# An attention and SSD encoder layer on one core: gated attention written over its gate, V in places of its own, decays loaded in halves, a new order in each head, and the first output step's operands rounded earlier

## The reference, cut to what matters

```python
h = rmsnorm(x, pre_norm_g)
proj = h @ w_in                      # 2048 -> 13376 columns: q, k, v, z_attn, z_ssm, x/B/C, dt
o = dilated_attention(q, k, v, rel_bias_table)          # 16 heads x 128
attn_out = rmsnorm(o, attn_norm_g) * silu(z_attn)
ssm_out = ssd_branch(z_ssm, xbc, dt_raw, ...)           # 32 heads x 64, both directions
mix = concatenate([attn_out, ssm_out]) @ w_out
y = x + rmsnorm(mix, post_norm_g)
```

## Time and profile before

| what | us |
|---|---|
| runs, median (lowest to highest) of 3 | 2471.28 (2469.89 to 2485.74) |
| the profiled execution's own time | 2472.09 |
| its span in the profile | 2470.3 |
| PE busy | 2409.2 (98%) |
| DVE busy | 1786.7 (72%) |
| ACT busy | 995.1 (40%) |
| mean granted TensorE clock | 0.993 of full |

### The profile page before, as it was taken

One profiled execution on the slowest core, in us unless ns is written; L12 is line 12 of the kernel. 1 busy time (PEld: TensorE's weight loads), 2 busy tenths in 40 slices (PEclk: granted clock), 3 DMA queues, 4 the chain that ended last, 5 costly groups with the idle time before them and its releaser, 6 DMA issues. The chain is left out here.

```text
span 2470.3 us, 36360 instructions
## 1 busy us (share of the span) xinstructions
PE 2409.2 (98%) x13604; PEld 2280.5 (92%) x13604; DVE 1786.7 (72%) x2563; ACT 995.1 (40%) x1664; POOL 466.1 (19%) x750
## 2 busy tenths in 40 slices
PE   7999999999999999999999999999999999999998
PEld 7999999999999999999998889899889888888887
DVE  5676766666666677777758778777878768777867
ACT  6333433333333333333335455454545532333332
POOL 0000277777773011111100000000000000000000
PEclk9999999999999999999999999999999999999999
DMA  5235466666665344443474555556555435445544
GB/s 167 72 112 182 126 198 206 204 205 200 200 199 158 114 128 132 127 125 119 122 242 145 184 184 160 182 179 193 156 192 167 139 133 170 151 156 130 175 160 164
DMA packets 318345, 398.81 MB, mean 161 GB/s; under 512 B 22822, under 2 KB 238310, under 8 KB 315287
## 3 DMA queue, kind: packets, MB, share of 16 engines
q1 hardware_dynamic: 266103, 225.20, 29.8%
q0 software_dynamic: 29168, 95.62, 12.2%
q10 hardware_dynamic: 22960, 76.53, 9.0%
HBM read 309.02 MB, written 95.59 MB: 164 GB/s over the span
## 5 line engine op out<-in xcount | busy, mean ns | idle before, releaser
L1166 PE MATMUL ps<-h_hi,w_hi 128*128 128x384 f32 x1088 | 365.2, 336 | 0.0
L1166 PE MATMUL ps<-h_lo,w_hi 128*128 128x384 f32 x1088 | 365.0, 335 | 0.0
L1166 PE MATMUL ps<-h_hi,w_lo 128*128 128x384 f32 x1088 | 364.6, 335 | 0.0
L2443 DVE TENSOR_TENSOR w_lo<-raw_qk,w_hi 128x512 fp32r<-128x512 f32 x272 | 214.3, 789 | 154.6 <-ACT w_hi L1696 153.2
L1166 PE MATMUL ps<-t_hi,w_lo 128*128 128x384 f32 x816 | 276.0, 338 | 0.0
L1166 PE MATMUL ps<-t_hi,w_hi 128*128 128x384 f32 x816 | 275.6, 338 | 0.0
L1166 PE MATMUL ps<-t_lo,w_hi 128*128 128x384 f32 x816 | 275.0, 337 | 0.0
L1696 ACT ACTIVATE w_hi<-raw_qk 128x512 fp32r<-128x512 f32 x272 | 171.2, 630 | 244.7 <-PE ps L1166 244.7
L1030 PE MATMUL ps<-h_hi,w_hi 128*128 128x384 f32 x768 | 205.2, 348 | 0.0
L1166 PEld LDWEIGHTS ps<-h_lo,w_hi 128*128 128x128 f32 x1088 | 204.3, 188 | 0.0
L1166 PEld LDWEIGHTS ps<-h_hi,w_lo 128*128 128x128 f32 x1088 | 204.2, 188 | 0.0
(11 more groups left out here) (370 smaller groups left out, 5411.9 us busy)
## 6 DMA issues: line engine op xcount, KB each, us to landing
raw_qk<-in_w_in SPq DMA_DIRECT2D x102, 512.0 KB, 4.3
w_raw<-in_w_in SPq DMA_DIRECT2D x144, 256.0 KB, 3.5
stage<-loc_scr ACTq DMA_DIRECT2D x16, 1536.0 KB, 11.9
stage<-t_scr SPq DMA_DIRECT2D x48, 512.0 KB, 3.8
stage<-zx_scr ACTq DMA_DIRECT2D x61, 384.0 KB, 5.2
stage<-in_w_out SPq DMA_DIRECT2D x36, 512.0 KB, 3.7
stage<-in_w_in SPq DMA_DIRECT2D x34, 512.0 KB, 4.2
zx_scr<-w_raw SPq DMA_DIRECT2D x34, 384.0 KB, 3.3
```

Source lines behind the costliest of these rows:

```text
L1166: ins = nc.tensor.matmul(ps[:, bank, 0:HALF_T], w, h(k), start=(start and kk == 0 and q == 0), stop=(last and kk == KC - 1 and q == 2), sk ...
L2443: nc.vector.tensor_tensor(w_lo[:, n_slot(n, pp), :], src, w_hi[:, n_slot(n, pp), :].bitcast(f32), ALU.subtract).then_inc(w_lo_done, 1)
```

## The change

It has five parts.

1. `attention_gated` writes its product over the gate `za` instead of over `oT`, and `store_att` stores `za`. The wait of `biased_maxima` for `ua_stored` goes. The load of the next `za` moves from `load_head` to `load_behind_scores`, behind a wait for `ua_stored`.
2. V is loaded in two halves into places of its own, and a head earlier, behind `v_rounded`.
3. The decays are loaded in two halves, one for each direction: the second half behind `silu_of_gates` of the head before (it waits for `wmat_done`, when that half of `decay` has been used), the first still behind `within_chunks`.
4. The order in a head: on PE `scores` stand one half earlier, two halves instead of one stand between `turn_probs` and `turn_probs_of_sample`, and three instead of two between `turn_v` and `across_chunks`. ACT and DVE are reordered to match.
5. The first output step: the `u` parts are rounded once the last gate tile's first chunk has been used, the weight pieces after its third, and the squares, `square_added`, `attention_gated` and `across_read` change places around them.

```diff
+        v_part = (sq_c[:, P:P + HALF_T], loc_ssum[:, TT * 64:TT * 64 + HALF_T])
...
-                pool.dma_start(u_scr[a * P:(a + 1) * P, :], oT).then_inc(ua_stored, 16)
+                pool.dma_start(u_scr[a * P:(a + 1) * P, :], za).then_inc(ua_stored, 16)
...
             def head(a):
-                stream_halves(a, 1, 2)
+                stream_halves(a, 1, 1)
                 scores(a)
                 scores_of_sample(a)
-                stream_halves(a, 3, 4)
+                stream_halves(a, 2, 4)
                 turn_probs(a)
-                stream_halves(a, 7, 1)
+                stream_halves(a, 6, 2)
                 turn_probs_of_sample(a)
                 attend(a)
+                stream_halves(a, 8, 1)
                 turn_x(a)
-                stream_halves(a, 8, 2)
                 if a < LAST:
                     turn_v(a + 1)
-                stream_halves(a, 10, 2)
+                stream_halves(a, 9, 3)
                 across_chunks(a)
...
-            def load_decays(a):
-                act.dma_start(decay.rearrange("p (d n) -> p d n", d=2),
-                              loc_scr.rearrange("(d h) t -> d (h t)", d=2)[:, a * 2 * T:(a + 1) * 2 * T]
+            def load_decays(a, d):
+                if a > 0 and d == 1:
+                    act.wait_ge(wmat_done, a)
+                act.dma_start(decay[:, 2 * T * d:2 * T * (d + 1)].rearrange("p (o n) -> p o n", o=1),
+                              loc_scr.rearrange("(d h) t -> d (h t)", d=2)[d:d + 1, a * 2 * T:(a + 1) * 2 * T]
                               .partition_broadcast(P)).then_inc(decay_in, 16)
...
-                load_decays(a)
-                if a < LAST:
-                    act.wait_ge(att_gated, a)
-                    load_zx(za, ZX_ZA, a, za_in)
+                load_decays(a, 0)
...
                     if a > 0:
+                        act.wait_ge(ua_stored, 16 * a)
+                        load_zx(za, ZX_ZA, a, za_in)
...
             def biased_maxima(a):
                 dve.wait_ge(strip_in, 16 * a + 16)
-                if a > 0:
-                    dve.wait_ge(ua_stored, 16 * a)
...
-                nc.vector.tensor_tensor(oT, oT, za, ALU.mult).then_inc(att_gated, 1)
+                nc.vector.tensor_tensor(za, oT, za, ALU.mult).then_inc(att_gated, 1)
```

More of the change, by code:

```diff
@@ L1636, in sample_rounded, with load_v @@
                 nc.scalar.activation(pTs_hi[:, :], ps[:, 4, :], ACT.Copy).then_inc(pts_out, 1)
[L1638 to L1641, removed]
+            def load_v(i):
+                for half in range(2):
+                    act.dma_start(v_part[half], zx_scr[(ZX_V + i) * P:(ZX_V + i + 1) * P,
+                                                       half * HALF_T:(half + 1) * HALF_T]).then_inc(v_in, 16)
             def attended(a):
@@ L1826, in head @@
                 probs_rounded(a)
+                exp_of_decays(a)
                 sample_rounded(a)
[L1828 to L1839, removed]
                 if i % 2:
                     k_rounded(i)
+                stream_hi(m + 2)
+                attended(a)
+                attended_sample(a)
+                squared(a)
+                stream_hi(m + 3)
+                x_turned(a)
+                v_rounded(i)
+                if a > 0:
+                    load_xs(i)
+                if i < LAST:
+                    load_v(i + 1)
+                if i % 2 == 0:
+                    q_rounded(i)
+                silu_of_gates(a)
+                load_decays(i, 1)
                 stream_hi(m + 4)
-                silu_of_gates(a)
+                stream_hi(m + 5)
                 if i % 2:
                     q_rounded(i)
-                stream_hi(m + 5)
-                if i % 2 == 0:
+                else:
                     k_rounded(i)
@@ L1869, in split_first_parts, with first_w2_rounded @@
                                      scale=mix_cols[:, kt:kt + 1]).then_inc(m_hi_done, 1)
+            def first_w2_rounded(k):
+                act.wait_ge(w2_in[0], 16)
+                nc.scalar.activation(w2_hi[0][:, k * NBW:(k + 1) * NBW], w2_first[:, k * NBW:(k + 1) * NBW], ACT.Copy
+                                     ).then_inc(w2_piece_hi, 1)
             load_head(LAST)
@@ L1876, in _ @@
             probs_rounded(LAST)
+            exp_of_decays(LAST)
             sample_rounded(LAST)
-            exp_of_decays(LAST)
             square_first(1)
             square_first(2)
+            last_gate_used(0)
+            for k in range(GRP):
+                first_u_rounded(k)
             attended(LAST)
+            attended_sample(LAST)
+            x_turned(LAST)
+            act.wait_ge(ua_stored, 16 * LAST)
             tile_ready(tile_of("za", LAST))
             tile_into(tile_of("za", LAST), parity_of("za", LAST), za, ACT.Silu)
-            x_turned(LAST)
-            attended_sample(LAST)
             squared(LAST)
+            last_gate_used(2)
+            for k in range(GRP):
+                first_w2_rounded(k)
             square_first(3)
             act.wait_ge(tile_done, tile_of("zs", LAST) + 1)
-            for k in range(GRP):
-                split_first_parts(k)
-                if k == 0:
-                    act.wait_ge(usq_added, 3)
-                    tile_into(tile_of("zs", LAST), parity_of("zs", LAST), zs, ACT.Silu)
+            act.wait_ge(usq_added, 3)
+            tile_into(tile_of("zs", LAST), parity_of("zs", LAST), zs, ACT.Silu)
             w2_split(1)
@@ L2596, in head @@
                 probs_lo(a)
-                if i % 2 == 0 and a < LAST:
-                    q_lo_of(i)
-                stream_lo(m)
+                stream_lo(m + 1)
+                if a == LAST:
+                    first_square()
                 sample_lo(a)
-                stream_lo(m + 1)
-                stream_lo(m + 2)
                 weighted_decays(a)
+                if a < LAST:
+                    square_added(a)
+                weights_in_chunks()
+                if a == LAST:
+                    add_square_first(1)
+                    add_square_first(2)
                 scaled_x(a)
                 if a == LAST:
-                    weights_in_chunks()
                     return
                 v_lo_of(i)
-                square_added(a)
-                weights_in_chunks()
+                if i % 2 == 0:
+                    q_lo_of(i)
+                stream_lo(m + 2)
                 stream_lo(m + 3)
@@ L2642, in split_first_parts, with first_w2_lo @@
                     m_hi[0][:, k * T:(k + 1) * T].bitcast(f32), ALU.mult, ALU.subtract).then_inc(m_lo_done, 1)
-            dve.wait_ge(u_first_in, 16)
-            nc.vector.tensor_tensor(ssum, u_first[0], u_first[0], ALU.mult).then_inc(usq_added, 1)
-            add_square_first(1)
-            add_square_first(2)
+            def first_w2_lo(k):
+                dve.wait_ge(w2_piece_hi, k + 1)
+                nc.vector.tensor_tensor(w2_lo[0][:, k * NBW:(k + 1) * NBW], w2_first[:, k * NBW:(k + 1) * NBW],
+                                        w2_hi[0][:, k * NBW:(k + 1) * NBW].bitcast(f32), ALU.subtract
+                                        ).then_inc(w2_piece_lo, 1)
+            for k in range(GRP):
+                first_u_lo(k)
+                first_w2_lo(k)
             square_added(LAST)
             attention_gated(LAST)
+            across_read(LAST)
             add_square_first(3)
-            for k in range(GRP):
-                split_first_parts(k)
-            across_read(LAST)
             skip_added(LAST)
```

42 lines of the change are left out of this document (21 added, 21 removed).

## The result

The changed kernel takes 2501.07 us (median of 4 runs, 2487.48 to 2506.45), the kernel before 2471.32 beside it (4 runs, 2469.89 to 2485.74): ratio 1.0098, interval 1.0051 to 1.0144. It is about 1% slower, where 2429 was forecast, and lies outside the range of 2422 to 2448.

A forecast was written before the change was run, and what follows sets the result against it. PE, busy 98% of the span, was taken to lose time only by 39.3 us of waits and a lowered clock. Gains of 35.7 and 12.3 made 48.0, less 6 paid back, net 42: 2429.3 us, range 2422 to 2448.

The forecast's parts named there:

- I take 7: Decays' load in the head loop: a 768 KB half was taken to land 7 us after issue, against 8.9 of cover.
- it may take the whole load's 11.3: Decays' load: the upper bound for the half's landing, 11.3 us, as head 10's whole load took from issue to use.
- The prediction's own sign of being wrong: Head loop: the forecast is wrong if decays land after 9 us, or if scores wait over 1 us in most heads.
- The first half lands no sooner than the whole did: Rival at DVE's `decay_differences`: waits of 2.4 us in 15 heads, more beside `cb`, 2482 us; deciding landing 11.3; chance 0.05.
- The gate store, 10.0: Sample's scores in odd heads: 7 waits for the maxima, held by the store of `oT`, would go, gaining 10.0 us.
- V, 2.1: `turn_v`: five of six waits would go, gaining 2.1 us; head 0's 3.6 stays, within 1 us either way.
- Decays in halves, 17.5: `turn_probs`: with decays loaded in halves, PE's waits for `normalised`, 17.5 us, would all go.
- Order in the head: Head loop: `attend`'s 2.2 us of waits go; `scores` may wait for `y_summed`, 2 us in all, bounds 0 and 15.
- 0 to 0.5: Sign at `scores`: a wait of 0 to 0.5 us was expected in the changed profile.
- First output step, 3.9: First output step: PE's wait goes, gaining 3.9 us, or 0 if the weights' load came 4 us later.
- The clock, 12.3: Stretches at a lowered clock after PE's stops: all 12.3 us come back; with stops of 1 us, up to half stays lost.
- The sum: Whole kernel: 35.7 us of waits and 12.3 of clock make 48.0; less 6 paid back, net 42.

The follow-up runs named there:

- e1: The kernel after, with the strips of heads 2 to 15 stored ahead of the head loop instead of in it: 2422.89 us, ratio 0.9775.
- e11: e1 run once more, as the base for e9 and e10: 2420.89 us.
- e2: The kernel after, with the same strip stores issued in the middle of the head, behind the strip and gate loads: 2428.69 us, ratio 0.979.
- e12: The kernel after, with each strip store made of 4 heads by 16 rows instead of 2 by 32: 2424.26 us, ratio 0.9794.
- e4: The kernel before, with the strips of heads 2 to 15 stored ahead of the head loop as in e1: 2470.38 us, ratio 0.9968.
- e10: e1 with the old gate store, `oT` stored and the maxima waiting for it: 2421.47 us.
- e8: e1 with both halves of the decays issued together behind `within_chunks`: 2462.99 us, ratio 0.995.
- e9: e1 with the first output step's operands rounded in the old order: 2424.56 us.
- e6: The kernel after, with the strip stores issued behind the SSD input, V and the decays' second half: 2456.72 us, ratio 0.992.

## Why the prediction was wrong

*The model of the wait was right, one input was not.* The step that failed is "I take 7" for the half load's landing, with its upper bound "it may take the whole load's 11.3". The half that counts, the first, took 13.5 at the median, and up to 17.0, and the bound was no bound. So PE's wait, put at nothing, was 56.0 us. The prediction's own sign of being wrong, decays that land after 9 us, came true. The term was sized by bytes and by the earlier trace rows; what stands ahead on the issuing queue was in no term, though the change puts four loads (SSD input, V's two halves, the second half of the decays) right behind the strips' stores. Even with the stores away the 7 was low for this half: it takes 8.6 in e1 and 7.3 in e11, and up to 10.3. That it is near 7 over both halves (6.9 and 6.5) is because the second ones take about 6.2.

*The rival that ends slower was right in place, not in reason, size or chance.* "The first half lands no sooner than the whole did" had 0.05 and 2482; its deciding point of 11.3 us was passed by 2, and the time by 19. Its reason, other queues' traffic, is not what e2 and e12 show: it is ACT's own queue, and then the DMA engines behind it.

*The gate store, 10.0.* The wait is gone, as said. But e4 loses it without this edit, and e10 has the old store at no cost. The 10.0 us were the strips' too: with them gone from the loop DVE has no wait for that store in either. That GpSimd's store of 384 KB took 8.2 (row of before above) and ACT's load of as much 5.2 should have raised the question.

*V, 2.1.* `turn_v` waits no more, but head 0's wait did not stay there: it moved to `scores`, 6.0 us for V's low part, a loss of 2.4 outside the bound of 1. One issue is the reason. ACT in the kernel after:

```profile
1271.74 7.52 ACTq L1643 DMA_DIRECT2D sq_c<-zx_scr  x1
...
1280.40 0.81 ACT L1414 ACTIVATE k_hi<-ps 128x768 fp32r<-128x768 f32 x1 [9.21 <-issue]
```

V of head 1, a load ahead that nobody needs yet, was issued there right behind the strips and held ACT for 7.52 us, where such an issue takes 0.45 in head 4. `k_hi` waited for it, and DVE's low parts of k and V came behind `k_hi`.

*Decays in halves, 17.5.* The term holds only with the strips away. In e1 DVE still waits 19.1 us for them in 14 heads, but PE only 1.3. The halves pay when the queue is clear: e8 against e1, 40 us.

*Order in the head.* `scores` waits 3.7 us for `y_summed`, 0.46 in 8 heads, where 2 was taken and "0 to 0.5" named; the same in e1. `attend` waits no more.

*First output step, 3.9.* No wait after; e9 puts it at 2.5 to 3.7.

*The clock, 12.3.* It was taken as length times what is missing, and for the kernel before that was nearly right, since PE worked through most of the slow stretches. In the kernel after it stood through many of them. By stretch, kernel after (columns as in the earlier trace rows):

```profile
1333.00:1377.00 44.00, 43.88 (x286) 42.05 (x284) 34.47 (x56) 22.96 (x42) 2.92 (x5) 1.00 0.56 172
1377.00:1421.00 44.00, 38.61 (x244) 36.50 (x244) 34.47 (x56) 20.22 (x33) 2.35 (x4) 0.96 0.52 155
1470.00:1490.00 20.00, 11.83 (x60) 11.52 (x59) 11.16 (x16) 6.66 (x10) 0.00 (x0) 0.74 0.40 144
```

The last is the stop of head 4: 0.74 while PE works 11.83 of 20. The lower level is half of the full clock, so half of its length is lost. Summed over the trace that is 35.2 us in the kernel after, 21.9 of it in time that PE works; before it is 18.7, with 14.9 of it in such time; in e1 8.8, with 5.1. So the clock gave 9.8 us back in e1 and cost 7.0 more in the kernel after. PE's busy time in e1:

```profile
span 2421.5 us, 36380 instructions
...
PE 2391.9 (99%) x13604; PEld 2272.1 (94%) x13604; DVE 1797.3 (74%) x2563; ACT 998.2 (41%) x1664; POOL 466.7 (19%) x750
```

It is 17.3 us less than before, and the waits are 32.0 less (39.3 less 7.3): together 49.3 for a span shorter by 48.8. Of the 17.3 the clock explains 9.8. The other 7.5 were in no term. They lie mostly in these groups, counted without the clock's share: 3.3 in `attend`, 2.2 in `turn_v`, 1.8 in the sample's scores, 0.8 in `turn_probs`, with 1.7 more in `scores`. The kernel after, whose busy time grew by only 1.0 in spite of 7.0 more from the clock, has the most of that gain too. Why these groups are shorter no run shows; waits that the profile counts as busy would do it.

*The sum.* 42 was near for a kernel whose strips are out of the way, where e4 to e1 shows 47.5, but partly by luck: the half load was low by 1 to 2 us, the 10.0 for the gate store was not its own, and the 7.5 stood nowhere.

What stays open: how an engine shares its time between ACT's pieces and those of other queues. SP's weights have 14 quick steps and two late ones as well (in head 4 the last two of one chunk after 10.9 and 12.1 us, of another after 23.7 and 25.2), but no run took the transfers of GpSimd or SP away.

## What to carry to other kernels

When a change moves loads, write down the whole issue order of the queue that they join, with the shape of each transfer ahead. A transfer whose outermost dimension is small occupies few DMA engines for long, and a wider load behind it on that queue waits for its few pieces on those engines; reshape it, or put it where nothing urgent follows. Bound a load's landing by what stands ahead of it, not by the time that it took in another place. Read it for each load by itself: a median over two loads of one line hid that the first halves were the slow ones in e6, and loads that share a semaphore get each other's steps. Count a low clock only where the engine works.

## What the runs showed of the hardware that was not expected

- 224 KB stored with an outermost dimension of 2 keep about two packets under way: the packets of two such stores last 9.2 to 11.8 us, and with 4 they last 5.0 to 5.5. Turning 2 into 4 took 77 us off the kernel (2501.07 to 2424.26, on chips where before took 2471.32 and 2474.27).
- A load of 384 KB issued right behind the two stores had 14 of its 16 steps after 3.3 us and the last two after 14.2 and 14.3; behind stores with 4 the last four came after 6.5 to 6.9, and with no store ahead all came by 3.2.
- A 768 KB broadcast that DVE waits for takes 7.3 to 8.6 us with the stores away (e11, e1) and 13.5 with them ahead. The figures of the Trainium skill (DMA: Bandwidth & Descriptors, anatomy of one DMA), a fit to DMAs issued from GpSimd, give 3.8 as an estimate; no run here shows so little (the least is 4.1, in e9).
- The delay reaches other queues: SP's 256 KB of weights took 11.8 us instead of 3.6, GpSimd's 384 KB store 8.2 in the kernel before and 4.2 in e1.
- One DMA issue on ACT took 7.52 us right behind the stores, at a time when the DMA engines were over 90% busy; 162 of ACT's 175 issues in that kernel took 0.66 us or less, and the others 0.67 to 2.8.
